# Turns of dilated heads in a bank of their own: the fourth score bank joins 15 groups later

## Chip, cores and metric

One NeuronCore of one Trainium2 chip runs the whole program. The metric is the device time of one execution in microseconds; it is given as the median of several runs. The engines are TensorE (PE, with its weight loads as PEld), VectorE (DVE), ScalarE (ACT), GpSimd (POOL) and the queue of SyncE (SP), which issues all DMAs.

## What is computed

Two blocks over one sequence of 512 tokens of width 1024, in float32. The first block is a gated linear recurrence layer and a sliding-window attention layer. The second block, in which the change lies, is a mixer of three kinds of attention heads and an MLP:

```python
a_q, a_kv, a_g, b_qkv, c_qkv = jnp.split(proj, PROJ_SPLITS, axis=-1)
o_a = nsa_mixer(...)            # 4 heads: compressed, selected and window attention, gated and summed
o_b = dilated_mixer(b_qkv...)   # 6 heads, merged into 2: dilations 1, 4 and 16
o_c = stick_breaking_mixer(c_qkv...)   # 6 heads, weights from a reversed running sum
x = x + jnp.concatenate([o_a, o_b, o_c], -1) @ w_out
x = x + jnp.square(jax.nn.relu(rms_norm(x, norm_mlp) @ w_up)) @ w_down
```

The dilated mixer first normalises queries and keys per head: `q = rms_norm(qkv[:, :, 0], qk_gain[0])`, `k = rms_norm(qkv[:, :, 1], qk_gain[1])`. Bringing these twelve tiles (queries 0 to 5, keys 0 to 5) into the layout of the scores is the work that the change moves.

## The kernel before

**The attention of the second block** is a software pipeline of 68 groups, one per step i. A group is one head (batch) and one block of 128 queries; `attention_two` (L237) lays out their order: eight groups of stick-breaking heads, then the compressed and selected and window groups mixed with the remaining stick-breaking groups up to 43, and from group 44 the string LATE (L154): `n` for a selected or window group of the second pair, `D` for a dilated one. The dilated groups are 46, 48, 51, 53, 56, 58, 61 and 63, each with three score strips (one for each dilation); all others have one strip.

Each engine runs its own loop over the steps, and semaphores tie them together. In step i PE does, in this order (`pe_part`, L830 to L863): the scores of group i+4 (L769, from group 44 on only after the values), the transposes of the probabilities of group i (`turn`, L785), the product with the values of group i-1 (L805), a turn of a finished pair (`pair_turn`, five steps after its end), a turn of a dilated tile, and, up to step 29, a piece of a projection (G1, G2, G3: L1298 to L1300). ACT's step (L928 to L953) begins with the four functions of a stick-breaking group i+3 (`soft1`, L878 to L885), then the copy of the dilated tile turned in step i-1 (L944), the exponential of group i+2 (`masked`, L904), its share of the copies of turned probabilities (L926) and the last exponential of a stick-breaking group (`soft2`, L921). DVE masks the scores (L1036), does the running sum of the stick-breaking groups (L1050, then L1051, which frees the score bank), its share of the copies (L970), the scaling at the end of a batch (L1111, L1116) and the two halves of a finished pair (L1140, L1141).

**PSUM banks.** There are eight. Score strips go in turn over the banks 0, 1 and 2; bank 7 is the fourth score bank, which joins when group WIDE_FROM (L162) is placed (`place_strips`, L577); until then the pieces of the projections use it. The scores of a strip wait until the strip before it in its bank has been read (L755). Turned probabilities go in chunks of up to four 128x128 blocks to bank 3 (even chunk) or 4 (odd chunk); even chunks are copied by DVE, odd ones by ACT. Turns of pairs and of dilated tiles are chunks too, numbered in one row with the rest (`with_chunks`, L275; `turn_chunk`, L823). A chunk c waits until chunk c-2 has been taken from its bank. Banks 5 and 6 hold the outputs.

**Dilated tiles.** TURNS2 (L152) gives the twelve steps in which PE turns a tile. Numbered k = 0 to 11 in that order, tile k goes through four engines' instructions: POOL makes it double-width and scaled (`double`, L1206) in one of two buffers, PE turns it (L827), ACT copies it back to the same buffer (L944), and POOL splits it into a high part (L1216) and a low part (L1219). POOL's own order is written out: double(0), double(1), split(0), double(2), split(1), double(3) and so on (L1222). split(0) also waits for the end of the last piece of G3 (L1215), since it writes over tiles that the pieces read. The scores of the first dilated group wait for six splits, those of group 56 for twelve (L751).

Before and after this pipeline stand the projections and outputs, in which PE multiplies 128x512 tiles in threes (L1298 to L1300); POOL (or DVE) splits each weight unit for them.

Of the kernel before, what the change touches and what calls it, by code (L numbers as in the profile page):

```python
# [26 lines left out]
P = 128  # L27
# [88 lines left out]
for _name, _n in [("rg", NG * 3 * NRG), ("g_a", KD), ("g_kv", KD), ("g_b", KD), ("g_mix", KD), ("g_mlp", KD),  # L116
# [32 lines left out]
ITEMS1 = {-3: ("gate", 4, 8), 14: ("gate", 5, 6), 30: ("gate", 6, 6), 46: ("gate", 7, 6)}  # L149


TURNS2 = dict(zip((28, 30, 31, 33, 34, 36, 37, 39, 40, 42, 43, 45),  # L152
                  [("q", 0), ("q", 2), ("q", 4), ("k", 0), ("k", 2), ("k", 4), ("q", 1), ("q", 3), ("q", 5), ("k", 1), ("k", 5), ("k", 3)]))
LATE = "nnDnDnnDnDnnDnDnnDnDnnnn"  # L154

# [3 lines left out]
TAKEN = {PIECE_STEPS[name][2 * t + 1] + 1: (name, t) for name in PIECE_STEPS for t in range(TB)}  # L159
GATES_AT = PIECE_STEPS["G1"][-1] + 1  # L160
SCALES_AT = PIECE_STEPS["G2"][-1] + 6
WIDE_FROM = 36  # L162
F6_HIGH, F6_LOW = 5, 6
TURN_LAG, OUT_LAG = 5, 6

# [134 lines left out]
def two_block_kernel(nc, x_d, weights_d, params_d, tables_d, swa_d, ident_d, out_d):  # L300
    BANK, FREE, BEFORE, LAST_USE = plan()
    ctx = ExitStack()
    with ctx:
# [3 lines left out]
        def sem(name):  # L307
            return ctx.enter_context(nc.semaphore(name))
# [98 lines left out]
        tanh_done = sem("tanh_done")  # L407
        piece_done = sem("piece_done")
        gates_raw, gates_exp = sem("gates_raw"), sem("gates_exp")
        scale_step, scale_ask, scale_root = sem("scale_step"), sem("scale_ask"), sem("scale_root")  # L410
        root_log = sem("root_log")
        heads_split = sem("heads_split")
# [154 lines left out]
        def make_attention(a):  # L567
# [84 lines left out]
            if a == 2:  # L652
                for p, end in enumerate(pairs):
                    extra.setdefault(end + TURN_LAG, []).append(("pair", p))
                for i, key in TURNS2.items():
                    extra.setdefault(i, []).append(key)
            chunk_of = with_chunks(groups, batches, 2 if a == 1 else 4, extra)

            place_strips()
# [1 line left out]
            def chunk_ready(c):  # L661
                return s["pt_ready"], c + 1
# [78 lines left out]
            def pe_part(pe, item, tail, behind_scores=None):  # L741
                def scores(i):
                    g = groups[i]
                    b, n = batches[g["b"]], g["n"]
                    kind = b["kind"]
                    if n == 0 and kind == "stick":
                        pe.wait_ge(heads_split, 2 * (b["head"] // 2) + 2)
                    if n == 0 and kind == "cmp":
                        pe.wait_ge(evac_a, FREE[("kcT", 0)][1])
                    if n == 0 and kind == "dil":  # L750
                        pe.wait_ge(dil_split, 6 * (b["head"] + 1))  # L751
                    for k, w in enumerate(g["w"]):
                        st = g["strip0"] + k
                        if strip_before[st] is not None:
                            pe.wait_ge(*strip_read(strip_before[st]))  # L755
                        elif a == 2:
                            who, value = LAST_USE[strip_bank[st]]
                            pe.wait_ge(FREESEM[who], value)
                        if kind == "cmp":

                            for h in range(4):
                                mm = pe.matmul(score_bank(st)[:, 32 * h:32 * h + 32], q_stack(h)[:, n * P:(n + 1) * P].bitcast(F32),
                                               kcT[:, 0:32], start=h == 0, stop=h == 3, skip_group_check=True)
                            mm.then_inc(s["scores"], 1)
                            continue
                        terms = scores_ap(g, k)
                        for t, (q, kk) in enumerate(terms):
                            out = score_bank(st)[:, 0:w]
                            mm = pe.matmul(out, q, kk, start=t == 0, stop=t == len(terms) - 1 and kind != "stick")  # L769
                        if kind == "stick":  # L770

                            mm = pe.matmul(score_bank(st)[:, w - P:w], idm[:, 0, :], idm[:, 1, :], start=False, stop=True)
                        mm.then_inc(s["scores"], 1)
# [36 lines left out]
                def pair_turn(p):  # L810
# [9 lines left out]
                        mm = pe.transpose(B[7][:, t * P:(t + 1) * P], otok[:, slot[p], t, :], ident[:])  # L820
                    mm.then_inc(s["pairT"], 1)

                def turn_chunk(key, src):  # L823
                    c = chunk_of[key]
                    pe.wait_ge(*chunk_taken(c - 2))
# [4 lines left out]
                for i in range(-LOOK - 1, ng + OUT_LAG):  # L830
# [12 lines left out]
                    if i - TURN_LAG in pairs:  # L843
                        pair_turn(pairs.index(i - TURN_LAG))
                    if a == 2 and i in TURNS2:
                        k = DIL_ORDER.index(TURNS2[i])
                        pe.wait_ge(dil_doubled, k + 1)
                        turn_chunk(TURNS2[i], doubles[k % 2])
                    if i in part_at:
                        key, q, parts = part_at[i]  # L850
                        if q == 0 and before7[key]:
# [13 lines left out]
            def act_part(act, item, behind_scores=None):  # L865
# [62 lines left out]
                for i in range(-LOOK, ng + OUT_LAG):  # L928
# [9 lines left out]
                        item(("scales", 0))  # L938
                    if a == 2 and i - 1 in TURNS2:
                        name, m = TURNS2[i - 1]  # L940
                        act.wait_ge(*chunk_ready(chunk_of[name, m]))
                        src = B[3 + chunk_of[name, m] % 2][:]
                        scale = hsc[:, 2:3] if name == "q" else par[:, PC["dil"] + 1:PC["dil"] + 2]
                        act.activation(doubles[DIL_ORDER.index(TURNS2[i - 1]) % 2].rearrange("p t q -> p (t q)"), src, ACT.Copy,  # L944
                                       scale=scale).then_inc(chunk_taken(chunk_of[name, m])[0], 1)
                    if 0 <= i + LOOK - 1 < ng:
                        masked(i + LOOK - 1)
                    if i == -1 and a == 2:
# [218 lines left out]
            def pool_part(pool):  # L1167
# [42 lines left out]
                def split_dil(k):  # L1210
                    name, m = DIL_ORDER[k]
                    src = doubles[k % 2].rearrange("p t q -> p (t q)")
                    pool.wait_ge(*chunk_taken(chunk_of[name, m]))
                    if k == 0:
                        pool.wait_ge(units_done, U_G3 + 4)  # L1215
                    pool.tensor_scalar(dil_tile(name, m, 0), src, 1.0, 1.0, ALU.mult, ALU.mult).then_inc(dil_high, 1)  # L1216
# [1270 lines left out]
```

## Time and profile before

| | us |
|---|---|
| median of 3 runs | 1145.75 |
| lowest and highest | 1144.41, 1146.90 |
| profiled execution, its own time | 1148.03 |
| profiled execution, its span | 1146.2 |
| PE busy in it | 1103.4 (96%) |
| DVE, ACT, POOL busy in it | 620.6, 428.8, 531.5 |

In the rows below, times are from the start of the span. A busy time of PE is the sum of instructions whose ends are modelled; PEclk is the granted clock as a share of 2.4 GHz. A name in square brackets behind an instruction is the engine, tile and line that released it, ahead of it stands the time for which its engine was idle. `arena` is the big buffer in SBUF in which the tiles of this stage lie, `bank` is any PSUM bank. A group of instructions on one row (x4, x8) starts at the time shown. A transpose or a value product of 128x128 float32 takes one row per pass, so a block of values shows as x2.

### The profile page before, as it was taken

What the parts mean: (1) busy time and instruction counts of PE and PEld (TensorE: products, weight loads), DVE (VectorE), ACT (ScalarE), POOL (GpSimd) and SP (SyncE); (2) the same over time, 40 slices, a digit from 0 to 9 for tenths busy, and PEclk for the clock granted to TensorE, in tenths of its full rate; (3) what the DMA queues carried; (4) which work ended last, traced back from release to release, by engine and by line L of the source; (5) the groups of instructions that cost most, each with busy time, mean ns of one, the idle gap of its engine ahead of it and who ended that gap; (6) DMA issues with size and microseconds to landing.
All of it is one profiled execution on the core that took longest, in us unless ns stands there. A gap on an engine that the chain in (4) does not pass through costs nothing.

```text
span 1146.2 us, 16119 instructions
## 1 busy us (share of the span) xinstructions
PE 1103.4 (96%) x5801; PEld 943.6 (82%) x5801; DVE 620.6 (54%) x1102; ACT 428.8 (37%) x878; POOL 531.5 (46%) x533
## 2 busy tenths in 40 slices
PE   6999999999989999999999888999999999999998
PEld 5788888888869998888798877888878888888887
DVE  6869686768556764656655567756531321321321
ACT  5374758363335651213565575532110200210210
POOL 0000000000342434979833668219966776776772
PEclk9999999999999999999999998899999999999999
DMA  6322322313220101333301200103323222322221
GB/s 253 125 94 87 116 92 93 129 55 124 93 78 19 38 20 37 112 109 114 127 26 49 74 1 20 56 2 128 119 83 105 97 92 94 103 96 91 93 92 53
DMA packets 27279, 97.18 MB, mean 85 GB/s; under 512 B 3024, under 2 KB 3408, under 8 KB 27088
## 3 DMA queue, kind: packets, MB, share of 16 engines
q1 hardware_dynamic: 27216, 96.32, 24.7%
q8 instruction: 41, 0.67, 0.2%
q14 instruction: 22, 0.18, 0.1%
HBM read 94.21 MB, written 2.10 MB: 84 GB/s over the span
## 4 chain that ended last, share of the span: by engine, by line
PE 69%; DVE 9%; issue 9%; POOL 7%; ACT 5%; DMA 0%; POOLq 0%; SPq 0%; DVEq 0%; ACTq 0%
PE bank L1298 20%; PE bank L1300 19%; PE bank L1299 19%; PE bank L805 4%; PE bank L769 3%; POOL wl L1251 3%; POOL wh L1248 2%; PE bank L785 2%; DVE arena L2026 1%; DVE wl L1977 1%; POOL wl L1250 1%; ACT wh L1657 1%; POOL hold L1247 1%; DVE arena L2361 0%; DMA x<-x_in 0%
## 5 line engine op out<-in xcount | busy, mean ns | idle before, releaser
L1247 POOL TENSOR_TENSOR hold<-hold 128x2 f32<-128x2 f32 x117 | 29.7, 254 | 522.9 <-PE bank L1300 522.9
L1298 PE MATMUL bank<-xh,wh 128*128 128x512 f32 x568 | 227.1, 400 | 10.8 <-DVE xl L1946 8.7
L1300 PE MATMUL bank<-xh,wl 128*128 128x512 f32 x568 | 222.7, 392 | 0.0
L1299 PE MATMUL bank<-xl,wh 128*128 128x512 f32 x568 | 222.7, 392 | 0.0
L1298 PE MATMUL bank<-yh,wh 128*128 128x512 f32 x520 | 203.4, 391 | 2.9 <-DVE yl L2366 2.4
L1300 PE MATMUL bank<-yh,wl 128*128 128x512 f32 x520 | 202.4, 389 | 0.0
L1299 PE MATMUL bank<-yl,wh 128*128 128x512 f32 x520 | 202.3, 389 | 0.0
L1251 POOL TENSOR_TENSOR wl<-raw,wh 128x512 fp32r<-128x512 f32 x117 | 173.6, 1484 | 0.0
L1250 POOL TENSOR_TENSOR wl<-raw,wh 128x512 fp32r<-128x512 f32 x117 | 158.4, 1354 | 9.8
L1298 PEld LDWEIGHTS bank<-xh,wh 128*128 128x128 f32 x568 | 107.6, 189 | 33.9 <-issue 10.9
L1300 PEld LDWEIGHTS bank<-xh,wl 128*128 128x128 f32 x568 | 107.5, 189 | 23.0
L1248 POOL TENSOR_SCALAR wh<-raw 128x1024 fp32r<-128x1024 f32 x117 | 125.5, 1072 | 0.0
L1299 PEld LDWEIGHTS bank<-xl,wh 128*128 128x128 f32 x568 | 107.7, 190 | 21.5 <-issue 0.7
L1298 PEld LDWEIGHTS bank<-yh,wh 128*128 128x128 f32 x520 | 97.6, 188 | 24.4 <-DVE yl L2366 3.2
L1300 PEld LDWEIGHTS bank<-yh,wl 128*128 128x128 f32 x520 | 97.6, 188 | 20.6
L1299 PEld LDWEIGHTS bank<-yl,wh 128*128 128x128 f32 x520 | 97.6, 188 | 19.8
L1910 ACT ACTIVATE arena<-arena 128x512 f32<-128x512 f32 x32 | 20.2, 633 | 244.8 <-DVE arena L2361 244.8
L2373 DVE TENSOR_TENSOR x<-bank,x 128x512 f32<-128x512 f32 x32 | 22.1, 691 | 140.8 <-PE bank L1300 140.8
L805 PE MATMUL bank<-arena 128*128 128x64 f32 (+1 forms) x620 | 89.3, 275 | 3.5 <-ACT arena L926 1.9
L1977 DVE TENSOR_TENSOR wl<-raw,wh 128x1024 fp32r<-128x1024 f32 x56 | 68.0, 1222 | 40.1 <-ACT wh L1657 39.7
L805 PEld LDWEIGHTS bank<-arena 128*128 128x128 f32 x620 | 83.9, 200 | 6.1 <-ACT arena L926 2.3
L1298 PE MATMUL bank<-wh,xh 128*128 128x512 f32 (+2 forms) x224 | 84.7, 378 | 3.8 <-POOL wl L1251 2.9
(257 smaller groups left out, 1806.6 us busy)
## 6 DMA issues: line engine op xcount, KB each, us to landing
raw<-weight_units SPq DMA_DIRECT2D x173, 512.0 KB, 3.4
x<-x_in SPq DMA_DIRECT2D x4, 512.0 KB, 7.1
out_fm<-x SPq DMA_DIRECT2D x8, 256.0 KB, 2.0
arena<-tables SPq DMA_DIRECT2D x1, 1024.0 KB, 10.7
par<-params SPq DMA_DIRECT2D x1, 166.0 KB, 2.4
arena<-swa_table SPq DMA_DIRECT2D x1, 128.0 KB, 11.3
ident<-identity SPq DMA_DIRECT2D x1, 64.0 KB, 8.3
```

The lines of the kernel that those rows point to most:

```text
L769: mm = pe.matmul(out, q, kk, start=t == 0, stop=t == len(terms) - 1 and kind != "stick")
L785: mm = pe.transpose(B[3 + c % 2][:, j * P:(j + 1) * P], probs_of(i, strip)[:, kb * P:(kb + 1) * P], ident[:])
L805: mm = pe.matmul(out, pt[:, c % slots, j * P:(j + 1) * P], value_ap(g, s_, kb), start=first, stop=total == 0)
L1247: pool.tensor_tensor(hold[:], hold[:], hold[:], ALU.add).then_inc(held, 1)
L1248: pool.tensor_scalar(wh[:, j, :], raw[:, j, :], 1.0, 1.0, ALU.mult, ALU.mult).then_inc(high_done, 1)
L1250: pool.tensor_tensor(wl[:, j, 0:512], raw[:, j, 0:512], wh[:, j, 0:512], ALU.subtract)
L1251: pool.tensor_tensor(wl[:, j, 512:1024], raw[:, j, 512:1024], wh[:, j, 512:1024], ALU.subtract)\
L1298: pe.matmul(out, lh, rh, start=start, stop=False)
L1299: pe.matmul(out, lh, rl, start=False, stop=False)
L1300: return pe.matmul(out, ll, rh, start=False, stop=stop)
L1977: dve.tensor_tensor(wl[:, u % RING, :], raw[:, u % RING, :], wh[:, u % RING, :], ALU.subtract)\
L2373: dve.tensor_tensor(x[:, m, :], B[4 + m % 4][:], x[:, m, :], ALU.add).then_inc(down_read, 1)
```

## The change

The twelve turns of dilated tiles leave the row of chunks and go to bank 7, with two semaphores of their own (`dil_turned`, `dil_copied`): turn k waits for the copy of turn k-1, turn 0 for the last reader of a G3 piece. In return bank 7 joins the score banks only from group 51 on and not from group 36; groups 36 to 50 use banks 0, 1 and 2. The steps of the turns change from 28, 30, 31, 33, 34, 36, 37, 39, 40, 42, 43, 45 to 30, 31, 32, 34, 35, 36, 38, 39, 40, 42, 43, 45. The tiles' order stays. ACT's copy stays in the step after the turn. As the chunks are renumbered, the split of the copies between DVE and ACT differs for twelve of the groups 29 to 45, and is the same again from group 46 on.

```diff
-TURNS2 = dict(zip((28, 30, 31, 33, 34, 36, 37, 39, 40, 42, 43, 45),
+TURNS2 = dict(zip((30, 31, 32, 34, 35, 36, 38, 39, 40, 42, 43, 45),
-WIDE_FROM = 36
+WIDE_FROM = 51
+        dil_turned, dil_copied = sem("dil_turned"), sem("dil_copied")
@@ make_attention
-                for i, key in TURNS2.items():
-                    extra.setdefault(i, []).append(key)
@@ scores
                         if strip_before[st] is not None:
                             pe.wait_ge(*strip_read(strip_before[st]))
+                        elif a == 2 and strip_bank[st] == 7:
+                            pe.wait_ge(dil_copied, len(DIL_ORDER))
@@ pe_part
+                def dilated_turn(k):
+                    pe.wait_ge(dil_doubled, k + 1)
+                    if k == 0:
+                        pe.wait_ge(FREESEM[LAST_USE[7][0]], LAST_USE[7][1])
+                    else:
+                        pe.wait_ge(dil_copied, k)
+                    for t in range(TB):
+                        mm = pe.transpose(B[7][:, t * P:(t + 1) * P], doubles[k % 2][:, t, :], ident[:])
+                    mm.then_inc(dil_turned, 1)
...
-                        k = DIL_ORDER.index(TURNS2[i])
-                        pe.wait_ge(dil_doubled, k + 1)
-                        turn_chunk(TURNS2[i], doubles[k % 2])
+                        dilated_turn(DIL_ORDER.index(TURNS2[i]))
@@ act_part
-                        act.wait_ge(*chunk_ready(chunk_of[name, m]))
-                        src = B[3 + chunk_of[name, m] % 2][:]
+                        act.wait_ge(dil_turned, DIL_ORDER.index(TURNS2[i - 1]) + 1)
+                        src = B[7][:]
...
-                                       scale=scale).then_inc(chunk_taken(chunk_of[name, m])[0], 1)
+                                       scale=scale).then_inc(dil_copied, 1)
@@ pool_part, split_dil
-                    pool.wait_ge(*chunk_taken(chunk_of[name, m]))
+                    pool.wait_ge(dil_copied, k + 1)
```

## Rows read from the trace of the kernel before

**Rows 1.** The page: span of the profiled execution.
```profile
span 1146.2 us, 16119 instructions
```
**Rows 2.** Busy time by stretch: PE, PEld, DVE, ACT, POOL; then PEclk, DMA share, GB/s.
```profile
666.00:709.00 43.00, 35.28 (x246) 32.62 (x244) 30.05 (x76) 29.72 (x80) 36.07 (x36) 0.88 0.00 1
...
755.00:820.00 65.00, 65.00 (x298) 53.41 (x298) 35.32 (x42) 12.29 (x20) 50.80 (x49) 1.00 0.27 89
```
**Rows 3.** Who waited for whom, 660 to 720 us: total, times, longest.
```profile
POOL xh L1216 <- PE bank L1300: 15.8, 1, 15.8
...
PE bank L827 <- POOL arena L1206: 3.4, 3, 1.6
...
PE bank L785 <- DVE yl L1141: 2.5, 2, 1.8
...
PE bank L827 <- ACT arena L944: 2.3, 2, 1.8
```
**Rows 4.** Timeline of PE, steps 30 to 45: turns of dilated tiles (the first with a pair's).
```profile
666.96 1.04 PE L827 MATMUL bank<-ident,arena 128*128 128x128 f32 x8
...
670.27 0.63 PE L827 MATMUL bank<-ident,arena 128*128 128x128 f32 x4 [0.53 <-ACT arena L944]
...
674.16 0.66 PE L827 MATMUL bank<-ident,arena 128*128 128x128 f32 x4 [0.90 <-POOL arena L1206]
...
683.62 0.66 PE L827 MATMUL bank<-ident,arena 128*128 128x128 f32 x4 [1.55 <-POOL arena L1206]
...
691.48 1.09 PE L827 MATMUL bank<-ident,arena 128*128 128x128 f32 x4 [1.81 <-ACT arena L944]
...
705.12 0.60 PE L827 MATMUL bank<-ident,arena 128*128 128x128 f32 x4
```
**Rows 5.** Timeline of POOL: split(0), split(1), double(3), double(8), and the last split's high part.
```profile
666.02 0.65 POOL L1216 TENSOR_SCALAR xh<-arena 128x512 fp32r<-128x512 f32 x1 [15.75 <-PE bank L1300]
...
670.22 0.62 POOL L1216 TENSOR_SCALAR xh<-arena 128x512 fp32r<-128x512 f32 x1 [1.07 <-ACT arena L944]
670.92 2.06 POOL L1219 TENSOR_TENSOR xh<-arena,xh 64x512 fp32r<-64x512 f32 x1
673.05 1.05 POOL L1206 TENSOR_TENSOR arena<-arena,v 128x512 f32<-128x512 f32 x1
...
689.29 1.05 POOL L1206 TENSOR_TENSOR arena<-arena,v 128x512 f32<-128x512 f32 x1
...
706.53 0.62 POOL L1216 TENSOR_SCALAR yh<-arena 128x512 fp32r<-128x512 f32 x1 [1.56 <-ACT arena L944]
```
**Rows 6.** All low parts of dilated tiles on POOL (L1219): durations min/median/max in ns.
```profile
L1219 POOL TENSOR_TENSOR xh<-arena,xh x7: 1263/1282/2057, 666.8 to 695.8; 64x512 fp32r<-64x512 f32 x6, 128x512 fp32r<-128x512 f32 x1
```
**Rows 7.** Timeline of DVE: the running sum of group 34; the mask of group 47.
```profile
670.35 1.56 DVE L1050 TENSOR_TENSOR_SCAN arena<-arena 128x512 f32<-128x512 f32 x1
...
702.34 0.56 DVE L1036 CUSTOM_DVE_ANT_0 arena<-bank,arena 128x384 f32<-128x384 f32 x1
```
**Rows 8.** Timeline of ACT: dilated copies of steps 31 and 40; soft1 of group 41.
```profile
669.46 0.67 ACT L944 ACTIVATE arena<-bank,hsc 128x512 f32<-128x512 f32 x1
...
683.40 0.49 ACT L878 ACTIVATE arena<-bank 128x384 f32<-128x384 f32 x1
...
690.66 0.67 ACT L944 ACTIVATE arena<-bank,hsc 128x512 f32<-128x512 f32 x1
```
**Rows 9.** Busy time by stretch, as rows 2: between the turns, and the slow stretch.
```profile
668.00:692.00 24.00, 16.52 (x127) 14.54 (x126) 17.58 (x36) 18.41 (x47) 20.80 (x21) 0.97 0.00 1
...
691.40:701.40 10.00, 9.92 (x48) 9.95 (x49) 5.92 (x16) 4.48 (x11) 8.16 (x8) 0.52 0.01 2
```
**Rows 10.** Timeline of PE: value products of four blocks, inside and behind the slow stretch.
```profile
699.74 1.60 PE L805 MATMUL bank<-arena 128*128 128x64 f32 x8
...
702.13 1.00 PE L805 MATMUL bank<-arena 128*128 128x64 f32 x8
702.94 0.72 PE L769 MATMUL bank<-xl,xh 128*128 128x256 f32 x4
```

## The prediction

> **What bounds the kernel now.** I read the page first: the span is 1146.2 us [rows 1], the profiled execution's own time 1148.03, so 1.83 us lie around the span. That execution is 2.3 us above the median of the runs, 1145.75; differences found in it are added to the median. Then the busy times by stretch: behind the attention stage PE is busy in every microsecond of 755 to 820 us, but in 666 to 709, where the dilated tiles are turned, it works 35.3 of 43 us at 0.88 of its clock [rows 2]. Whatever reaches the end of that stretch sooner or later moves all that follows, since the later work is the same chain with the same intervals. So only this stretch, and what it hands on, is to be worked out.
>
> The waits name its bounds: PE waited for POOL's doubling (L1206) in three turns and for ACT's copy (L944) in two; POOL had waited 15.8 us for the last piece of G3 [rows 3]. With the timelines this reads: tile 0 was turned in step 28, but POOL may split tile 0 only from 666.02, and from then POOL's chain (double, high, low) paces the turns: turn 3 at 674.16 and turn 6 at 683.62 start when the doubling ends [rows 4, 5]. The starts of double(3) and double(8) are 16.24 us apart, 3.25 us for each tile; the parts alone are 1.05 + 0.62 + 1.28 and short gaps, some 3.1 us. Turn 8, at 691.48, waits 1.81 us for ACT's copy of tile 7, which started at 690.66 [rows 4, 8]. Right there the granted clock drops: 691.4 to 701.4 runs at 0.52, that is, most of it at 1.2 GHz [rows 9].
>
> **The change part by part.** (Turn k means tile k; steps are counted as in the code.)
>
> 1. *Fewer waits for banks 3 and 4.* Turns still cost PE four transposes each, about 0.4 us from start to start, twelve before and after. What goes is the wait of a turned chunk on its neighbour. In step 31 PE waited for the pair's low half in DVE, one of two such waits of 2.5 us together, the longer 1.8 us [rows 3]: so 0.7 us. The longer one, in step 48, is between a pair's chunk and group 48, and stays. The 0.7 us is worth nothing: turn 1, now in step 31, must wait for the copy of tile 0 anyway (part 3).
>
> 2. *Turn 0 leaves step 28.* There PE was fully busy with pieces, so G3 ends 0.4 us sooner. Step 30 has the turn instead. Nothing remains.
>
> 3. *POOL's chain starts later.* Tile 0 is now turned in step 30 at about 667, and ACT copies it in step 31, in the place where it copied tile 1: at 669.46, behind soft1 of group 34, to 670.13 [rows 8]. ACT gains there the copy of turned group 30 (0.3 us) and is fed 0.4 us sooner; equal. POOL, which began split(0) at 666.02, begins it at 670.2, just where it began split(1) before [rows 5]. It loses the gap of 1.07 us that it had there, and is one whole tile late from then on. double(2) takes the place of double(3), 673.05 to 674.1. Turn 2, now in step 32, waits for that; PE has done step 32 at about 671.8, so it stalls some 2.3 us, the longest stall of the stretch. double(7) takes the place of double(8) and ends at 690.34, double(8) ends 3.1 us later, at 693.4. In between, steps hold 2.0 to 2.3 us of PE's work per tile against 3.1 to 3.25 of POOL's, so PE arrives early at turns 4 to 8 and the lateness neither grows nor shrinks. ACT's own path gives nearly the same: turn 5 waits for double(5) until 683.3, its copy ends at 684.5, and soft1 of group 41 starts at about 685.1 instead of 683.40. From soft1 of 41 to turn 8 before took 691.48 - 683.40 = 8.1 us [rows 4, 8]; so 693.2. Turn 8 starts at 693.2 to 693.4 instead of 691.48: **+1.7 us**.
>
> Here a rule is weighed. Split(1)'s low part took 2.06 us against a median of 1.28 [rows 6], with DVE's running sum of 1.56 us beside it from 670.35 [rows 7]; split(0) now meets the same sum at the same time, so I keep 2.06. The Trainium skill, SBUF — State Buffer, section "SBUF: two separate sides", says that an instruction of DVE with two SBUF inputs and one of GpSimd exclude each other for their whole length; the trace agrees, with 0.78 us. Without the collision turn 2 would come 0.8 us sooner, and turn 8 would be bound by ACT's path alone, which would give +1.6.
>
> 4. *Behind turn 8.* Before, turns 9 to 11 waited for nothing: PE was the slower one, with half the clock. With the same drop of the clock, PE needs as long as before from turn 8 to turn 11, so turn 11 moves from 705.12 to 706.8. double(11) is ready long before. The splits end 1.7 us later, at about 710; their first reader (group 46) needs only six, the next (group 56) is read past 724. Free.
>
> 5. *Three score banks for groups 36 to 50.* The scores of a group now wait until the third strip back is read, not the fourth. Tightest is group 48, whose third strip needs group 47's mask: that started at 702.34 and ended at 702.9, while PE began group 48's scores at 702.94 [rows 7, 10]. So no wait even on its first strip. For the single-strip groups the needed reader is a whole step back. Cost 0; bounds 0 and, should DVE be half a microsecond late in each of the five multi-strip places, 2.5 us.
>
> 6. *The copies change hands.* Of the turned groups 29 to 45 ACT takes six that DVE had (30, 33, 35, 39, 41, 45) and gives six (29, 32, 36, 38, 42, 44), the like in size; both engines are busy 30 of the 43 us [rows 2]. Cost 0, bounds -0.5 to +0.5.
>
> Sum: +1.7 us against 1148.03, or 1147.4 on the median. Bounds of the unknown terms: -0.5 and +3.
>
> **The rivals.**
>
> *Rival A, slower: the clock falls a second time, at turn 2.* For it: the new stall of 2.3 us there is longer than the 1.81 us before 691.4, and about 1.3 us of waiting for the copy of tile 0 stand close ahead of it. Against it: the stalls of 0.90 and 1.55 us at turns 3 and 6 passed at 0.97 mean clock [rows 4, 9]. Price: a value product of four blocks took 1.60 us inside the slow stretch and 1.00 behind it [rows 10], a factor 1.6. In 668 to 692 PE is busy 69% of the time [rows 9]; 10 us at half clock hold 6.9 us of work that becomes 11, and the copies return later, so the turns get 3.7 us apart instead of 3.1 in three tiles: about +2 us, with +1 and +3.8 as ends (3.8 is 10 - 10/1.6, where PE has no slack). Total +3.7, so 1149.5. It decides from the point where such a stall brings the clock down. The Trainium skill, TensorE: Matmul & The Clock Gate, section on HAM oscillation, tells that waits between bursts of matmuls bring the slow clock back; the row of 691.4 agrees.
>
> *Rival B, faster: the clock stays up at turn 8.* The wait there is as long as before, 1.5 to 1.8 us, but the 0.7 us stall just ahead of it in step 40 (chunk behind chunk) is partly gone, and the idle time lies spread over turns 7 and 8. Then PE is fed by POOL to the end: double(11) is done at 693.4 + 3 x 3.1 = 702.7, and turn 11 starts there instead of 705.12: -2.4 us, 1143.3. Nothing can be quicker than POOL here, unless earlier stalls shrink too; end -4.
>
> *Rival C: the three score banks do cost*, as in part 5: +1.7 + 2 = 1149.5. Speaks against it: no row with PE's L769 waiting between 668 and 755.
>
> *Rival D: nothing is seen*, as ACT's path, not POOL's, set the end and PE's own slack takes the lateness: 0, 1145.8. That is inside my case's range.
>
> **How the numbers follow.** A measurement of this kernel can tell about 0.2%, 2.3 us. My case (with D) 0.43, own range 1145 to 1148; A 0.27; B 0.21; C 0.05; 0.04 for unnamed things of either sign. Slower by over 0.2% (above 1148.0): A, C and the edge of my case, 0.35. Faster (below 1143.5): most of B and little else, 0.22. Same: 0.43. The range leaves out the outer ends of A and B: 1142.0 to 1151.0. The predicted time is my case's, 1147.4.
>
> **What would show it.** Right: turn 0 near 667, the first L1216 of the stage at 670.2 and not 666.0, turn 2 with a wait of about 2.3 us on POOL's L1206, POOL without a gap from there to double(8) at about 693, no L769 of PE waiting on DVE. The last turn is at 706.8 with the drop at turn 8, near 702.7 without, and at 708 or more with a drop at turn 2; the granted clock between 672 and 702 tells which. Wrong: if POOL's first split comes before 669, if turn 2 does not wait, or if PE waits on L1036 or L1051 ahead of scores 46 to 50.

## Result and profile after

| | before | after |
|---|---|---|
| median of 11 runs | 1147.0 | 1150.32 |
| lowest and highest | 1140.47, 1154.38 | 1148.08, 1151.92 |
| profiled execution, its own time | 1148.03 | 1150.97 |
| profiled execution, its span | 1146.2 | 1149.2 |

The ratio of after to before is 1.0036, 95% interval 1.0019 to 1.0053: slower, by 3.3 us between the medians and 4.1 us by the ratio. Twelve more runs of the unchanged text of after (`after_again`, below) gave 1.0054 (1.0029 to 1.0079). The forecast was 1147.4, 1.65 us above the median of 1145.75 known then and within 0.2% of it. The measured time lies inside the range of 1142.0 to 1151.0, almost at the time of Rival A (1149.5).

First the stretch where the tiles are turned, then smaller windows of it; columns as in [rows 2]. "Turn 2" is the turn of tile 2, as in the prediction.

```profile
666.00:709.00 43.00, 36.25 (x228) 34.53 (x227) 27.51 (x68) 28.30 (x72) 33.76 (x32) 0.76 0.00 1
668.00:692.00 24.00, 18.89 (x116) 17.61 (x114) 13.47 (x31) 16.14 (x42) 18.91 (x18) 0.79 0.00 1
...
672.00:674.00 2.00, 0.24 (x3) 0.10 (x1) 0.45 (x1) 1.34 (x5) 1.92 (x3) 0.81 0.00 0
674.00:676.00 2.00, 1.95 (x10) 1.95 (x11) 0.00 (x0) 0.80 (x2) 1.85 (x3) 0.50 0.00 0
...
682.00:684.00 2.00, 2.00 (x15) 2.00 (x13) 0.10 (x1) 0.78 (x3) 1.84 (x3) 0.63 0.02 4
684.00:686.00 2.00, 1.98 (x18) 1.71 (x15) 1.93 (x6) 0.69 (x1) 1.88 (x2) 1.00 0.00 0
...
694.00:696.00 2.00, 0.75 (x4) 0.76 (x5) 1.93 (x4) 1.80 (x4) 1.92 (x3) 0.50 0.00 0
```

The granted clock of 666 to 709 us is 0.76, against 0.88 in [rows 2], and that of 668 to 692 is 0.79, against 0.97 in [rows 9]. The small windows place the difference. In 672 to 674 PE works 0.24 of 2 us, and in that idle time the clock goes to its lower level (0.50, 1.2 GHz). It is back at 2.4 GHz only from about 683.5, some 10 us later. It falls again at about 693.7, ahead of turn 8, as it did before. PE's row looks busier than before (36.25 against 35.28 us) with fewer instructions (228 against 246): busy time at half clock is not more work.

Now the waits of 660 to 720 us, as in [rows 3] (L1226 is the split's high part, L954 ACT's copy, L832 the dilated turn, L1216 the doubling), and the timelines of PE and POOL, as in [rows 4] and [rows 5].

```profile
POOL xh L1226 <- ACT arena L954: 20.0, 1, 20.0
...
PE bank L832 <- POOL arena L1216: 5.2, 4, 1.8
...
PE bank L832 <- ACT arena L954: 1.5, 1, 1.5
```
```profile
667.54 0.60 PE L832 MATMUL bank<-ident,arena 128*128 128x128 f32 x4
...
670.47 0.63 PE L832 MATMUL bank<-ident,arena 128*128 128x128 f32 x4 [1.47 <-ACT arena L954]
...
674.05 1.11 PE L832 MATMUL bank<-ident,arena 128*128 128x128 f32 x4 [1.81 <-POOL arena L1216]
...
680.01 1.06 PE L832 MATMUL bank<-ident,arena 128*128 128x128 f32 x4
...
695.25 1.11 PE L832 MATMUL bank<-ident,arena 128*128 128x128 f32 x4 [1.53 <-POOL arena L1216]
```
```profile
670.41 1.11 POOL L1226 TENSOR_SCALAR xh<-arena 128x512 fp32r<-128x512 f32 x1 [19.98 <-ACT arena L954]
671.61 1.27 POOL L1229 TENSOR_TENSOR xh<-arena,xh 64x512 fp32r<-64x512 f32 x1
672.95 1.05 POOL L1216 TENSOR_TENSOR arena<-arena,v 128x512 f32<-128x512 f32 x1
...
676.01 1.05 POOL L1216 TENSOR_TENSOR arena<-arena,v 128x512 f32<-128x512 f32 x1
...
681.89 0.62 POOL L1226 TENSOR_SCALAR xl<-arena 128x512 fp32r<-128x512 f32 x1 [1.65 <-ACT arena L954]
...
694.08 1.11 POOL L1216 TENSOR_TENSOR arena<-arena,v 128x512 f32<-128x512 f32 x1
```

POOL's first split comes at 670.41 and not at 666.02; it had waited for ACT's copy of tile 0, as forecast. double(2) starts at 672.95 (forecast 673.05) and turn 2, behind it, at 674.05, after PE has idled for 1.81 us. The four transposes of turn 2 take 1.11 us instead of some 0.6: the clock had gone down inside that wait. Behind it PE, and no longer POOL, is the slow one: double(3) ends at 677.06, but PE at half clock gets to turn 3 only at 680.01, 5.96 us behind turn 2. The copies are late in turn, and at 681.89 POOL itself has waited 1.65 us for one, a gap that the forecast had excluded. Turn 8 starts at 695.25.

**A common clock for the comparisons.** Absolute positions differ by some tenths of a us before the stretch begins. So the start of DVE's running sum of group 29 serves as zero in every trace, and two marks are read from it: turn 8, and the first product of the output phase. Of before (first fence) and after (second):

```profile
654.46 0.69 DVE L1050 TENSOR_TENSOR_SCAN arena<-arena 128x256 f32<-128x256 f32 x1
...
755.14 0.47 PE L1298 MATMUL bank<-yh,wh 128*128 128x512 f32 x1
```
```profile
655.01 0.69 DVE L1060 TENSOR_TENSOR_SCAN arena<-arena 128x256 f32<-128x256 f32 x1
...
758.08 0.47 PE L1308 MATMUL bank<-yh,wh 128*128 128x512 f32 x1
```

Before: turn 8 at 37.02 (691.48 - 654.46), output at 100.68. After: turn 8 at 40.24, output at 103.07. Turn 8 is 3.22 us late and not 1.7, and the output 2.39 us. With the 0.55 us by which after is already late at zero, that is 2.94 us (758.08 - 755.14), which is the whole difference of the two profiled executions (1150.97 - 1148.03): from the output phase on nothing is added.

### The profile page after: what moved, and what is told of

The parts are those of the page before. It is cut to its first block, busy times and chain, and to the rows that moved or that the text cites. A ratio compares the mean times of both kernels' runs of the same rounds, so it can differ in the third digit from the quotient of the medians.

```text
span 1149.2 us, 16115 instructions
## 1 busy us (share of the span) xinstructions
PE 1106.5 (96%) x5801; PEld 947.3 (82%) x5801; DVE 620.5 (54%) x1102; ACT 429.9 (37%) x878; POOL 532.1 (46%) x533
## 4 chain that ended last, share of the span: by engine, by line
PE 71%; DVE 9%; issue 8%; POOL 7%; ACT 5%; DMA 0%; POOLq 0%; SPq 0%; DVEq 0%; ACTq 0%
PE bank L1308 20%; PE bank L1310 20%; PE bank L1309 20%; PE bank L806 4%; PE bank L770 3%; POOL wl L1261 3%; PE bank L786 2%; POOL wh L1258 2%; DVE arena L2036 1%; DVE wl L1987 1%; ACT wh L1667 1%; POOL wl L1260 1%; POOL hold L1257 1%; POOL arena L1216 1%; DMA x<-x_in 0%
```

## Experiments

After the first measurement (11 executions of either kernel) each version was run twelve times, in four sets, a to d, and each set has its own runs of the kernel before beside it on the same chip: 35, 29, 29 and 23. A ratio is taken within its set; medians of different sets are not compared directly. The mean clock is that of the whole span, averaged over the runs. The marks are in us from zero.

| run | set | median | ratio to before (95%) | mean clock | turn 8 | output |
|---|---|---|---|---|---|---|
| before | a | 1146.27 | 1 | 0.9916 | 37.02 | 100.68 |
| before | b, c, d | 1144.73, 1144.21, 1144.71 | 1 | 0.9937, 0.9936, 0.9936 | | |
| after | first | 1150.32 | 1.0036 (1.0019 to 1.0053) | 0.9865 | 40.24 | 103.07 |
| steps_only | a | 1149.01 | 1.0028 (1.0011 to 1.0045) | 0.9887 | 40.39 | 104.10 |
| late_bank_only | a | 1145.86 | 0.9989 (0.9971 to 1.0007) | 0.9930 | 37.04 | 95.16 |
| fill_turn2 | a | 1147.32 | 1.0022 (1.0004 to 1.0041) | 0.9921 | 38.43 | 100.36 |
| copy0_first | a | 1148.56 | 1.0025 (1.0011 to 1.0039) | 0.9878 | 37.97 | 100.73 |
| after_again | b | 1151.91 | 1.0054 (1.0029 to 1.0079) | 0.9864 | 38.50 | 100.41 |
| after_fill | b | 1144.52 | 0.9983 (0.9964 to 1.0002) | 0.9963 | 38.40 | 97.79 |
| before_fill | b | 1144.07 | 0.9983 (0.9959 to 1.0007) | 0.9955 | 37.05 | 95.08 |
| before_fill_all | c | 1139.84 | 0.9963 (0.9948 to 0.9977) | 0.9992 | 37.02 | 95.02 |
| after_fill_all | c | 1142.33 | 0.9980 (0.9966 to 0.9994) | 0.9993 | 38.46 | 96.86 |
| late_bank_fill_all | c | 1141.05 | 0.9967 (0.9951 to 0.9983) | 0.9988 | 37.00 | 94.99 |
| steps_only_fill_all | d | 1143.20 | 0.9985 (0.9971 to 0.9999) | 0.9987 | 38.71 | 97.23 |
| copy0_fill_all | d | 1142.87 | 0.9979 (0.9963 to 0.9994) | 0.9984 | 37.57 | 95.93 |

The marks are of one profiled execution each, those of before from the one of [rows 1]; the medians and ratios are of all runs. The second block's attention is one stretch; the clock falls elsewhere too, in some executions and not in others, so a single trace's total isn't the verdict.

### The parts alone

**steps_only**: the kernel before with the new steps, everything else as it was (turns in banks 3 and 4, WIDE_FROM 36).

```diff
-TURNS2 = dict(zip((28, 30, 31, 33, 34, 36, 37, 39, 40, 42, 43, 45),
+TURNS2 = dict(zip((30, 31, 32, 34, 35, 36, 38, 39, 40, 42, 43, 45),
```

> The kernel before with the new steps of the turns alone: chunks in banks 3 and 4 and the fourth score bank from group 36 stay. Theory (the later start of POOL's chain and the clock that falls at turn 2 are the loss): the same as the full change, +3 to +4.5 us over before; split(0) starts at 670 and not 666, turn 2 waits about 2 us on the doubling, the granted clock is 0.5 from about 673 to 683. Rival 1 (the three score banks of groups 36 to 50 are the loss): within 1 us of before. Rival 2 (the private bank, in which each turn waits for the copy of the turn before, is the loss): within 1 us of before.

Measured: 1.0028 (1.0011 to 1.0045), 1149.01. PE's timeline, turns 2 and 8, then POOL's first split and the window behind turn 2:

```profile
673.35 1.11 PE L827 MATMUL bank<-ident,arena 128*128 128x128 f32 x4 [2.11 <-POOL arena L1206]
...
694.40 1.11 PE L827 MATMUL bank<-ident,arena 128*128 128x128 f32 x4 [1.53 <-POOL arena L1206]
...
669.41 0.62 POOL L1216 TENSOR_SCALAR xh<-arena 128x512 fp32r<-128x512 f32 x1 [19.59 <-ACT arena L944]
...
673.00:683.00 10.00, 9.65 (x59) 9.62 (x60) 2.58 (x9) 5.99 (x17) 8.05 (x9) 0.66 0.00 1
```

The whole pattern of after is there without the bank: the stall before turn 2, the slow turn, the clock at 0.66 over the next 10 us (0.50 up to 680, not to 683 as expected), turn 8 at 40.39. By the ratio it is 3.2 us slower than before. Both rivals said within 1 us, so the slowdown comes from the steps. It is not shown that the private bank gains anything, either.

**late_bank_only**: the kernel before with the fourth score bank joining late, and nothing else.

```diff
-WIDE_FROM = 36
+WIDE_FROM = 51
```

> The kernel before with WIDE_FROM 51 alone. Theory: 0, between -0.7 and +0.7 us; the granted clock falls once, near 691, as before, and PE's scores wait for no mask. Rival 1 (three score banks are the loss): +2 to +4 us, with waits of PE's scores on DVE.

Measured: 0.9989 (0.9971 to 1.0007). PE's timeline and the two windows of the stretch:

```profile
674.69 0.33 PE L769 MATMUL bank<-yh,yl 128*128 128x128 f32 x1 [0.63 <-DVE arena L1051]
...
683.90 0.45 PE L769 MATMUL bank<-yh 128*128 128x384 f32 x1 [0.69 <-DVE arena L1051]
...
685.64 0.66 PE L827 MATMUL bank<-ident,arena 128*128 128x128 f32 x4 [0.59 <-POOL arena L1206]
...
666.00:709.00 43.00, 35.37 (x260) 32.16 (x259) 32.56 (x83) 30.23 (x81) 36.85 (x37) 0.96 0.00 1
709.00:755.00 46.00, 41.58 (x327) 38.04 (x325) 33.03 (x104) 23.24 (x72) 13.50 (x14) 1.00 0.14 47
```

Three score banks do make scores wait, for the running sums of two single-strip groups (0.63 and 0.69 us). Neither is in the multi-strip places where the prediction looked. Still they cost nothing, since PE would have waited a moment later anyway: the 1.55 us before turn 6 [rows 4] are 0.59 here. Turn 8 is at 37.04, against 37.02. In this execution the clock was at 0.96 in 666 to 709 (0.88 in [rows 2]) and at 1.00 from 709 on, so the output came at 95.16, 5.5 us sooner than in the trace of before. Taken alone, that would have made the late bank look like a gain that its ratio doesn't show.

### The clock at turn 2

**fill_turn2**: after, with twenty transposes that nobody reads, in the turn's own bank, between the wait for the bank and the wait for the doubled tile of turn 2.

```diff
-                    pe.wait_ge(dil_doubled, k + 1)
...
+                    for _ in range({2: 20}.get(k, 0)):
+                        pe.transpose(B[7][:, 0:P], ident[:], ident[:])
+                    pe.wait_ge(dil_doubled, k + 1)
```

> The changed kernel with 20 transposes of the identity into bank 7 (read by nobody) ahead of turn 2's wait for the doubling; they take about 2.2 us of the stall of 1.8 us. Theory: the clock stays at 2.4 GHz from 672 on, turns 3 to 7 wait again for POOL; 1.5 to 3 us faster than the changed kernel, so +1 to +2 over before, though the turn itself may come 0.4 us later. Rival (the lateness of POOL alone costs all of it, the slow clock lies in slack): no faster than the changed kernel, and +3.5 over before.

Measured: 1.0022 (1.0004 to 1.0041), 1147.32. Timeline and window:

```profile
671.05 2.35 PE L831 MATMUL bank<-ident 128*128 128x128 f32 x20
673.24 0.60 PE L834 MATMUL bank<-ident,arena 128*128 128x128 f32 x4
...
672.00:676.00 4.00, 4.00 (x39) 3.97 (x37) 1.17 (x5) 2.49 (x8) 3.84 (x4) 1.00 0.00 0
```

The filler takes the place of the idle time and of little else: turn 2 is at 19.20 from zero, in after at 19.04. The clock is 1.00 in 672 to 676 where after had 0.50 to 0.81, the turn takes 0.60 us and not 1.11, and turn 8 comes at 38.43 instead of 40.24. So in these two executions the fall at turn 2 cost 1.8 us at turn 8 (and 2.7 us at the output, 103.07 against 100.36), and the lateness that is left at turn 8 is 1.4 us. The mean clock of the twelve runs is 0.9921, like before's in its set (0.9916), and 0.0056 over that of after. In time the gain of this one filler is 0.0014 against the first measurement of after and 0.0032 against after_again, 1.6 to 3.7 us (1.5 to 3 expected), but the intervals overlap.

**copy0_first**: after, with ACT's copy of tile 0 put ahead of the stick-breaking functions of its step; the other copies stay behind them.

```diff
+                    if DIL_ORDER_AT(i) in (0,):
+                        turned_copy(i)
+                    if 0 <= i + LOOK < ng:
+                        soft1(i + LOOK)
...
+                    if DIL_ORDER_AT(i) not in (0,):
+                        turned_copy(i)
```

> The changed kernel, with ACT's copy of tile 0 ahead of the four functions of group 34 in step 31 and not behind them. Theory (POOL's late start is the root): split(0) starts at about 668 and not 670.4, every doubling 2.3 us sooner, the stall at turn 2 below 0.8 us and no fall of the clock there: 3 to 4.5 us faster than the changed kernel, -1 to +1 over before. Rival (the order of the copies is no matter, the loss is in the banks): within 1 us of the changed kernel, since ACT only swaps 0.6 us against 2.2.

Measured: 1.0025 (1.0011 to 1.0039), 1148.56. POOL's first split, a value product of PE, and the window at turn 2:

```profile
667.56 0.62 POOL L1235 TENSOR_SCALAR xh<-arena 128x512 fp32r<-128x512 f32 x1 [18.11 <-ACT arena L944]
...
670.55 0.66 PE L806 MATMUL bank<-arena 128*128 128x64 f32 x4 [1.55 <-ACT arena L936]
...
672.00:676.00 4.00, 3.47 (x17) 3.48 (x18) 2.31 (x6) 3.46 (x11) 3.74 (x5) 0.58 0.00 0
```

POOL's first split is at 13.94 from zero (15.40 in after), and turn 2 at 17.6 (19.04). That is 1.5 us sooner and not 2.3 as expected. And the functions that ACT had put off now hold up the copy of probabilities, so PE idles 1.55 us at the value product instead and 0.7 us at 672.5 on DVE's running sum, and the clock falls all the same, at 672.7. Moving the wait to another instruction doesn't help the clock. The fall here is short, though (0.99 over 676 to 680), and a long one begins at 689.7, just ahead of turn 8. The expectation, 3 to 4.5 us faster than after and level with before, was missed: by the ratios it is 1.3 to 3.3 us faster than after, and slower than before.

**after_again**: after, unchanged, to see whether the fall at turn 2 comes back.

> The changed kernel once more, as the control that shares its runs of before with the two kernels that follow: +2.5 to +4.5 us over before by every theory; the granted clock falls near 673 and near 694 in its profile.

Measured: 1.0054 (1.0029 to 1.0079), mean clock 0.9864 as in the first measurement. In the profiled execution the wait was there again, the fall short:

```profile
671.39 0.99 PE L832 MATMUL bank<-ident,arena 128*128 128x128 f32 x4 [1.80 <-POOL arena L1216]
```

By the ratio this is 6.2 us over before, more than the 2.5 to 4.5 expected. The profiled execution, at 1145.62, was one of the quick ones: ahead of turn 8 the clock was below 1 only from about 671.6 to 675, and turn 8 came at 38.50, as with the filler; it fell again at 692.1. So a wait of 1.8 us at the same place brings a fall of varying length. The four profiled executions with the new steps and no filler all have one here, in the stall (after, steps_only), just behind it (after_again), or behind the waits that took its place (copy0_first). It is long in the first two, some 10 and 7 us, and they lose 1.7 to 1.8 us by it at turn 8 (40.24 against 38.46, 40.39 against 38.71 with the clock held up, below). It lasts 3 to 4 us in the others and costs them 0.04 us (38.50 against 38.46) and 0.40 us (37.97 against 37.57).

### Filling the other stalls

**after_fill** adds to fill_turn2 fourteen transposes ahead of turn 8 and twelve ahead of the values of step 51, in a score bank whose strip has been read; **before_fill** is the kernel before with those two.

```diff
+                        filler(i, {40: (14, 'turn'), 51: (12, 'values')}[i][0])
```

> The changed kernel with filling transposes (identity, into a bank that nobody reads yet) in three stalls: 20 ahead of turn 2, 14 ahead of turn 8, 12 ahead of the values in step 51. Theory (clock and lateness add up): the clock stays at 2.4 GHz through turns 2 to 8, and what is left against the kernel before with its own fillers is the pure lateness of POOL's chain, +1 to +2.5 us. Against the changed kernel: 4 to 7 us faster. Rival (the fall of the clock costs nothing, since PE has slack there): within 1 us of the changed kernel.

> The kernel before with 14 filling transposes ahead of turn 8 and 12 ahead of the values in step 51. Theory: no fall of the clock near 691 and 721; the profiled stretch from turn 8 to turn 11 takes 10 us instead of 13.6; 3 to 6 us faster than before, and 1 to 2.5 us faster than the changed kernel with fillers. Rival (the fall is not caused by these stalls, or is in slack): within 1 us of before.

Measured: both 0.9983 (0.9964 to 1.0002, and 0.9959 to 1.0007). In the traces the filler does its work: the output is at 95.08 in before_fill and 97.79 in after_fill. Within this set after_fill is faster than after_again by 7.4 us between the medians (8.1 by the ratios, mean clock 0.9963 against 0.9864), before_fill faster than before by only 0.7 (1.9 by the ratio, 0.9955 against 0.9937). So after loses far more to the clock than before does, and the rival, that its fall costs nothing, is out; before_fill missed its 3 to 6 us. The two filled kernels come out level, though 1 to 2.5 us was expected between them: both still had falls at other places, and their intervals leave room for 2 us. The next three hold the clock up throughout this stage.

**before_fill_all, after_fill_all, late_bank_fill_all**: fillers at every place of this stage where PE had idled and the clock had fallen, in columns 384 to 511 of bank 5, which nobody reads. The places (step, ahead of what: how many) are the same six in all three, and one or more for the version's own stalls. The filler of step 0 also waits until the last user of bank 5 is done.

```diff
+                FILL = {(0, 'scores'): 14, (12, 'values'): 10, (23, 'piece'): 16, (40, 'turn'): 14, (48, 'chunk'): 14, (51, 'values'): 12, (37, 'turn'): 12}
+
+                def filler(i, place):
+                    for _ in range(FILL.get((i, place), 0) if a == 2 else 0):
+                        pe.transpose(B[5][:, 384:512], ident[:], ident[:])
```

That is before_fill_all; late_bank_fill_all is the same with WIDE_FROM = 51. after_fill_all has (31, 'turn'): 11 for (37, 'turn') and fillers of 20, 9 and 12 in bank 7 ahead of turns 2, 5 and 7.

> The kernel before with filling transposes (identity, into columns 384 to 511 of bank 5, which nobody reads) in all seven stalls of the attention stage of over 1.2 us (steps 0, 12, 23, 37, 40, 48, 51). Theory (the runs differ by how often the clock falls): mean granted clock 0.997 or more, 1140 to 1142 us, 4 to 6 us faster than before, and a smaller scatter between runs. Rival (the fillers only delay PE): no faster than the kernel before.

> The changed kernel with fillers in steps 0, 12, 23, 40, 48 and 51 as in the other, and ahead of turns 1, 2, 5 and 7. With the clock up in both, the difference to the kernel before with fillers is the pure price of the later POOL chain. My term of +1.4 to +1.7 us at turn 8: 0.7 to 2 us slower than that kernel. Rival (what is late at turn 8 is made good later, all the loss is the clock): within 0.5 us of it.

> The kernel before with WIDE_FROM 51 alone and the same fillers in steps 0, 12, 23, 37, 40, 48 and 51. Theory: the three score banks cost nothing, within 0.7 us of the kernel before with these fillers. Rival (they cost, hidden by the scatter of the clock): 1 to 3 us slower than it.

Measured: 0.9963, 0.9980 and 0.9967, intervals in the table. Of before_fill_all the anchor, the filler and turn 8 behind it, the first product of the output phase, and the two windows:

```profile
652.99 0.69 DVE L1064 TENSOR_TENSOR_SCAN arena<-arena 128x256 f32<-128x256 f32 x1
...
688.03 1.72 PE L746 MATMUL bank<-ident 128*128 128x128 f32 x14
...
690.01 0.63 PE L835 MATMUL bank<-ident,arena 128*128 128x128 f32 x4 [0.26 <-ACT arena L958]
...
748.01 0.47 PE L1312 MATMUL bank<-yh,wh 128*128 128x512 f32 x1
...
666.00:709.00 43.00, 36.76 (x295) 33.25 (x294) 32.40 (x81) 31.31 (x86) 38.97 (x39) 1.00 0.01 2
709.00:755.00 46.00, 44.18 (x339) 40.43 (x338) 32.86 (x103) 21.07 (x65) 9.91 (x10) 1.00 0.13 47
```

Of after_fill_all the same windows:

```profile
666.00:709.00 43.00, 39.53 (x323) 36.44 (x322) 30.69 (x77) 31.10 (x84) 36.89 (x37) 1.00 0.00 1
709.00:755.00 46.00, 43.87 (x348) 40.42 (x347) 32.84 (x100) 23.02 (x72) 13.23 (x14) 1.00 0.15 47
```

With the clock at 1.00 in this stage in all three, what remains is the schedule alone. Turn 8 is 1.44 us later in after_fill_all than in before_fill_all (38.46 against 37.02), the output 1.84 us (96.86 against 95.02), and the ratios differ by 0.0017, 2.0 us (the medians by 2.5; the twelve runs of the one lie between 1140.69 and 1143.12, of the other between 1138.23 and 1141.3). That is the upper end of the 0.7 to 2 us expected, and well over the rival's 0.5. The late bank costs nothing in the trace: 94.99 against 95.02. Its ratio is 0.9967 against 0.9963, 0.5 us, and its median 1.2 us higher; the scatter of twelve runs leaves up to about 1.5 us open.

The fillers are also worth more than anything in the change. before_fill_all runs at 1139.84 beside 1144.21 of before, the fastest of all versions here, and its twelve runs spread over 3 us, those of before beside it over 8 (1140.01 to 1148.03).

**steps_only_fill_all, copy0_fill_all**: the two remaining versions, at full clock. The first line is that of steps_only_fill_all, the other two are those of copy0_fill_all (the last one in bank 7).

```diff
+                FILL = {(0, 'scores'): 14, (12, 'values'): 10, (23, 'piece'): 16, (40, 'turn'): 14, (48, 'chunk'): 14, (51, 'values'): 12, (32, 'turn'): 20, (39, 'turn'): 12}
...
+                FILL = {(0, 'scores'): 14, (12, 'values'): 10, (23, 'piece'): 16, (40, 'turn'): 14, (48, 'chunk'): 14, (51, 'values'): 12, (31, 'values'): 12}
...
+                    for _ in range({2: 4, 4: 8, 7: 12}.get(k, 0)):
```

> The kernel before with the new steps alone, and fillers in steps 0, 12, 23, 32, 39, 40, 48 and 51. With the clock up, this tells the later steps from the private bank and the three score banks. Theory (the steps alone delay POOL's chain): 1.5 to 2.7 us slower than the kernel before with fillers (1139.8), that is near the changed kernel with fillers (1142.3). Rival (the private bank makes the delay): within 0.7 us of the kernel before with fillers.

> The changed kernel with ACT's copy of tile 0 ahead of soft1 of group 34, and fillers in steps 0, 12, 23, 31, 40, 48, 51 and ahead of turns 2, 4 and 7. Theory (the late first copy is what delays the chain): at full clock turn 8 comes about 1 us sooner than in the changed kernel with fillers, 0.5 to 1.5 us faster than it, 1141 to 1142. Rival (the delay is not in the first copy): the same as the changed kernel with fillers, 1142.3.

Measured: 0.9985 (0.9971 to 0.9999) and 0.9979 (0.9963 to 0.9994). The steps alone bring the output to 97.23, 2.2 us behind before_fill_all: all of the lateness, and 0.4 us more than with the private bank. By the ratios it is 0.0022, 2.5 us, behind before_fill_all, as the theory had it. Whether the bank takes back those 0.4 us can't be told from ratios of 0.9985 and 0.9980 out of different sets. With tile 0 copied first turn 8 comes 0.89 us sooner than in after_fill_all, as expected, and the output is at 95.93, so that 0.93 of the 1.84 us go with ACT's order in one step. But the expected gain in time is not seen (0.9979 against 0.9980), so this rests on single traces.

## Why the prediction was wrong

**The reading of the bound** held where the clock is up: POOL's chain paces the turns, and lateness there reaches the output phase.

**Parts 1 and 2** (fewer waits for banks 3 and 4, turn 0 out of step 28, both nothing): turn 0 came at 667.54 (about 667 forecast; on the common clock 12.53, 666.99 in the times of before), turn 1 waited 1.47 us for ACT's copy as said. steps_only, which keeps the turns in the row of chunks, has the same turn 8 as after within 0.3 us, clock falling or not (40.39 against 40.24, 38.71 against 38.46).

**Part 3** (POOL's chain later, +1.7 at turn 8) had the right mechanism and nearly the size: with the clock held up the lateness is 1.44 us. The stall at turn 2 was 1.81 us instead of 2.3. PE came to it when forecast (672.24 is 671.7 in the times of before, 671.8 forecast), but the doubling ended 0.65 us sooner than forecast (674.00 is 673.45, against 674.1): 0.35 us because the copy of tile 0 and with it the first split came sooner, the rest because the collision with DVE's running sum went otherwise. It did not hit the low part (2.06 us before, [rows 6]) but the high part, since the sum had started first this time (669.88 against 670.41; before, 670.35 against 670.22):

```profile
669.88 1.23 DVE L1060 TENSOR_TENSOR_SCAN arena<-arena 128x512 f32<-128x512 f32 x1
```

The high part, started at 670.41, took 1.11 us instead of 0.62, and the low part behind the sum's end 1.27. Both with the gap take 2.5 us, where the forecast had 2.8. The rule of the Trainium skill that was weighed (SBUF — State Buffer, section "SBUF: two separate sides") fits in the main: POOL's instruction is long while the sum runs, and no longer once it has ended. In both traces it is lengthened by 0.21 us less than the two overlap, though: by 0.49 us of 0.70 here, by 0.78 of 0.99 before.

**Part 4** (behind turn 8 nothing changes) roughly held. From turn 8 to the output the trace of before has 63.66 us, that of after 62.83, both with two falls of the clock; at full clock it is 58.00 and 58.40. So a fall there costs 2.2 to 2.8 us on average, and at full clock 0.4 us is added that the prediction didn't have; no run says by what. The last turn came at 708.05, as forecast for a drop at turn 2 (708 or more). The last split ended at 711.45 (about 710 forecast), and PE waited for none of them.

**Part 5** was priced right at 0 as far as late_bank_fill_all can tell, though its reasoning missed two waits of 0.6 to 0.7 us in single-strip groups (late_bank_only), which other waits absorbed. In after itself no score product of PE waited for DVE. **Part 6** was not tested by itself; its cost, if any, lies within the lateness at full clock.

**The step that failed** is in the weighing of Rival A and in "How the numbers follow". The sum had a new stall of 2.3 us at turn 2, but the likeliest case still put its cost in clock at nothing (0.43 for one drop of the clock, at turn 8, against 0.27 for a second one at turn 2). The argument was that stalls of 0.90 and 1.55 us had passed, and both are shorter than the new one. The runs showed a fall in that stall or soon behind it in all four profiled executions of versions with the new steps and no filler, and a mean clock of 0.9865 and 0.9864 in the two measurements of after, against 0.9937 for before beside the second. Where the fall lasted 10 us it cost 1.81 us at turn 8 (40.24 against 38.43), where it lasted 3 to 4 us it cost 0.04 and 0.40 us.

Rival A had the cause, and its price of about +2 us agrees with the 1.8 us of fill_turn2, but its way was another: it had three tiles 3.7 us apart, while turn 3 came 5.96 us behind turn 2, with PE and not the copies as the slow part. That its total of 1149.5 lies 0.8 us from the median of 1150.32 is partly luck, as the lateness was smaller than its 1.7, the fall has no fixed price, and before itself was 1.25 us slower in this measurement (1147.0) than the 1145.75 it was added to. Its cited rule, of TensorE: Matmul & The Clock Gate in the Trainium skill (section on HAM oscillation), tells of longer waits, for DMAs; the rows agree in kind, with a wait of 1.81 us for POOL: the clock went down inside the wait between two bursts, and PE got it back only some 10 us later.

**The sum as the runs give it.** The lateness is 0.0017, 2.0 us. The clock costs the kernel before 0.0037 (1 against 0.9963, 4.2 us) and after 0.0056 (1.0036 against 0.9980) to 0.0074 (by after_again), 6.4 to 8.5 us; so 2.2 to 4.2 us more than before. Together that is the measured 4.1 to 6.2 us, by the way it is worked out. These differences cross sets, and each ratio has an interval of some 0.0015 to 0.0025 on either side, so the split is an estimate; seen in traces are only the lateness at a full clock and the fall at turn 2. Nor do the two simply add up. On the line of time against mean clock through before's runs of the same set, the runs of after_again lie 0.5 us below it, while those of after_fill_all lie 1.8 us above theirs: at an equal mean clock the unfilled kernel shows no lateness. A likely reason, not shown by a run of its own, is that while PE works at half clock it is the slow one, and POOL's lateness is hidden behind it.

How much of the clock's cost belongs to turn 2 is open too. In the two traces of before and after the fall at turn 2 is the whole difference of the mean clock (0.990 and 0.985). But over the twelve runs of after_again the shortfall of 0.0073 is some 17 us more at half clock (2 x 0.0073 x 1146, an estimate), and the fall at turn 2 lasted 3 to 10 us in the traces; so other falls had a share.

**Rival B** (the clock stays up at turn 8) did not happen by itself; nearest to it is the trace of after_again, where turn 8 had the full clock and the fall came at 692.1, 1.2 us behind it. Forced by fillers in after_fill_all, it puts the output at 96.86 where before had 100.68. **Rival C** (the banks cost 2 us) finds no support in late_bank_fill_all: nothing in the trace, 0.5 us by the ratio. **Rival D** (nothing is seen) is refuted by the 1.84 us at the output and the 2.0 us in time, both at full clock.

Left open: why the clock fell for some 10 us in one execution of after and for 3 to 4 in another, with waits of 1.81 and 1.80 us. No run varied this alone.

## What to carry over

When a change puts a new stall of PE into a stretch that is not quite full, price the stall twice, once for itself and once for the clock that it may bring down; here the second was, by the estimate above, at least as dear as the first. Compare variants by their mean granted clock as well as by time, and hold the clock up with harmless transposes where only the schedule is to be judged. Such fillers, put where PE waits anyway, were worth more than the change: 0.9963 (0.9948 to 0.9977).

## What the hardware showed beside this

- Over the 35 runs of before in set a the time follows the mean granted clock with a correlation of -0.95: about 8.5 us for 0.01 of clock (0.988: 1149.3 to 1150.4 us; 0.991: 1145.8 to 1147.8; 0.995: 1141.9 to 1142.9; 0.999: 1140.8). About nine tenths of the variance between these runs go with the clock.
- A fall is tied neither to the length of one wait nor to its moment. Turn 2 of after waited 1.81 us, and the clock fell inside that wait. Turn 7 waited 1.60 us and still had the full clock behind it (its transposes took 0.66 us); the clock fell at 693.7, just as the wait of 1.53 us at turn 8 began. In after_again it fell 0.2 us behind the end of the wait at turn 2, and in copy0_first at 689.7, while PE was at work:

```profile
692.11 0.66 PE L832 MATMUL bank<-ident,arena 128*128 128x128 f32 x4 [1.60 <-POOL arena L1216]
```

- Which of the two is held up, POOL's instruction or DVE's running sum, went with which started first. A high part on POOL, with one tensor as its input, took 1.11 us instead of 0.62 when the sum (1.23 us) had started 0.53 us ahead of it; in before the high part started 0.13 us ahead and kept its 0.62, and the sum of the same size took 1.56.
